# Layer 0's query, attention-value and HGRN-gate projections as three products of halves, row by row of the weights

## The reference

```
(na_q, na_k, na_v, hq, hf, hb, hi, hg, ga, gh) = split_columns(h @ w_in)
slab of 512 columns:  0     1     2     3   4   5   6   7   8,9  10,11
o_na = neighbourhood_attention(rope(na_q), rope(na_k), na_v, context k and v)
o_hg = hgrn2_bidirectional(silu(hq), hi, gates from hf and hb)
y    = sigmoid(ga) * (o_na @ w_na_o) + sigmoid(gh) * ((rms_norm(o_hg) * silu(hg)) @ w_hg_o)
x    = x + g1 * (y @ w_out)
```

## Time and profile before

| what | value |
|---|---|
| median of 3 runs | 1620.96 us (1620.72 to 1624.62) |
| profiled execution, its own time | 1620.81 us |
| its span, first to last instruction | 1618.9 us |
| mean granted TensorE clock | 0.96 |
| PE busy | 1470.9 us, 91% |
| DVE, ACT, POOL busy | 853.9, 649.3, 239.4 us |
| norm and slab 3 on PE | 41.69 to 71.31 us |
| slab 2, rotations, slab 7 on PE | 249.71 to 308.1 us |
| layer 0 attention on PE | 308.2 to 385.4 us |

### The profile page before, as it was taken

The page is one execution under the profiler, slowest core; times in us unless marked ns, Lnnn a source line. Parts: engine busy times, 40 slices in busy tenths (PEclk is TensorE's granted clock), DMA queues, the critical chain, the costliest instruction groups (busy, mean ns, idle before and its releaser), DMA issues.

```text
span 1618.9 us, 17176 instructions
## 1 busy us (share of the span) xinstructions
PE 1470.9 (91%) x6712; PEld 999.4 (62%) x6712; DVE 853.9 (53%) x1153; ACT 649.3 (40%) x880; POOL 239.4 (15%) x210
## 2 busy tenths in 40 slices
PE   3999999998999958999999789999889988998884
PEld 1586665456888836888888478765558864433332
DVE  3367971676744456888888356870871132111003
ACT  3554431257233255778877365430350121111112
POOL 0006951300000001111210210660500000000000
PEclk9999999999999967999999889999999998999997
DMA  9511106394121546999999861116342466999991
GB/s 354 208 52 52 53 15 183 144 387 156 52 104 56 205 156 223 391 400 400 399 400 403 296 257 52 53 53 156 135 178 101 145 222 226 392 395 393 395 394 65
DMA packets 167144, 352.12 MB, mean 218 GB/s; under 512 B 21776, under 2 KB 22928, under 8 KB 167056
## 3 DMA queue, kind: packets, MB, share of 16 engines
q1 hardware_dynamic: 145472, 331.52, 55.1%
q0 software_dynamic: 3456, 12.58, 2.1%
q10 hardware_dynamic: 18128, 6.82, 2.1%
HBM read 339.38 MB, written 11.53 MB: 217 GB/s over the span
## 4 chain that ended last, share of the span: by engine, by line
PE 79%; DVE 8%; DMA 4%; issue 3%; POOL 3%; ACT 2%; SPq 0%; DVEq 0%; ACTq 0%; POOLq 0%
PE bank L1237 7%; PE bank L579 6%; PE bank L669 4%; PE bank L1259 4%; PE bank L989 4%; PE bank L986 4%; PE bank L995 3%; PE bank L590 3%; PE bank L615 3%; DMA ring<-in_w_in 2%; PE bank L806 2%; PE bank L809 2%; PE bank L802 2%; PE bank L1014 2%; PE bank L1024 2%
## 5 line engine op out<-in xcount | busy, mean ns | idle before, releaser
L2754 DVE TENSOR_TENSOR slab_lo<-slab,high 128x4096 fp32r<-128x4096 f32 x48 | 212.0, 4419 | 8.2 <-ACT high L1898 7.5
L1898 ACT ACTIVATE high<-slab 128x4096 fp32r<-128x4096 f32 x48 | 174.1, 3632 | 22.5 <-PE bank L995 14.5
L1237 PE MATMUL bank<-narrow_slab,picked 128*64 128x512 f32 x256 | 116.0, 607 | 12.0 <-issue 11.7
L1238 PE MATMUL bank<-narrow_slab,picked 128*64 128x512 f32 x256 | 116.2, 608 | 0.0
L2184 POOL DMA_INDIRECT feed_rows<-token_table,slot_token x16 | 40.6, 2538 | 504.5 <-DVE slot_token L2694 305.9
L669 PE MATMUL bank<-hT,ring 128*128 128x512 f32 (+1 forms) x256 | 102.8, 539 | 0.0
L579 PE MATMUL bank<-hT,ring 128*128 128x256 f32 (+1 forms) x384 | 99.6, 415 | 0.0
L579 PEld LDWEIGHTS bank<-hT,ring 128*128 128x128 f32 x384 | 72.9, 190 | 23.4 <-issue 15.1
L1237 PEld LDWEIGHTS bank<-narrow_slab,picked 128*64 128x64 f32 x256 | 35.2, 140 | 83.4 <-issue 82.8
L2920 DVE TENSOR_TENSOR hidden<-bank,gated 64x512 f32<-64x512 f32 x16 | 11.1, 695 | 121.1 <-ACT gated L2056 121.1
L1739 ACT ACTIVATE gsig<-bank 128x512 f32<-128x512 f32 (+1 forms) x32 | 15.7, 491 | 139.8 <-PE bank L579 69.9
(11 more groups left out here) (330 smaller groups left out, 3012.4 us busy)
## 6 DMA issues: line engine op xcount, KB each, us to landing
ring<-in_w_ada SPq DMA_DIRECT2D x24, 2048.0 KB, 13.3
ring<-in_w_in SPq DMA_DIRECT2D x24, 2048.0 KB, 8.8
slab<-in_w_gate SPq DMA_DIRECT2D x16, 2048.0 KB, 15.3
slab<-in_w_up SPq DMA_DIRECT2D x16, 2048.0 KB, 14.5
slab<-in_w_down SPq DMA_DIRECT2D x16, 2048.0 KB, 14.2
narrow_slab<-in_w_gate SPq DMA_DIRECT2D x16, 2048.0 KB, 17.4
narrow_slab<-in_w_up SPq DMA_DIRECT2D x16, 2048.0 KB, 22.0
narrow_slab<-in_w_down SPq DMA_DIRECT2D x16, 2048.0 KB, 19.2
```

The costliest lines, as they stand in the source:

```text
L1237: T.matmul(bank[0][0:64, :], x, gate[:, k, :], start=(k == 0), stop=(k == KT - 1))
L1238: mm = T.matmul(bank[0][64:128, :], x, up[:, k, :], start=(k == 0), stop=(k == KT - 1))
L1898: S.activation(half_of(e, kind)[:], w[:], ACT.Copy)\
L2754: V.tensor_tensor(low[:], w[:], half_of(e, kind)[:].bitcast(f32), ALU.subtract)\
```

## The change

In layer 0 slabs 3, 2 and 7 are now done by halves and by rows of the weights, as slab 6 was. Two functions hold the PE side, `tokens_by_halves` (slabs 6 and 2) and `features_by_halves` (slabs 3 and 7). Both open their four banks before the first product. The high rows lie in small buffers: 4 for slab 3, 4 for slab 2, 7 for slab 7.

- For slab 3, ACT and DVE now make a tile of `hT`, its high half, its low half, and the high and low half of the weight row, before they go on to the next tile. `levmask` moves ahead of the norm.
- `hT_hi` is made by ACT right after HGRN's last unit, and `hT_lo` by DVE before the rotations (in place over `hT`). The copies inside attention and ahead of the wide gates are gone, and `wide_gates` takes the tiles in plain order.
- DVE makes the low rows of slab 2 and the first three of slab 7 before the rotations, and the other five of slab 7 one each ahead of the first five rotations. ACT makes the last five high rows of slab 7 behind the four copies of slab 2's results.
- The 32 bias DMAs go from ACT's queue to SP's, ahead of the fill for the seventh ada slab, in both layers.
- Some buffers move: `ona`, `merged`, `pt`, `probs` 4 and 5. ACT waits for all eight heads of `bias` before its first write of `pt`, where DVE waited before it wrote `probs` 4 and 5.

```diff
+    query_row = [fixed(f"query_row{i}", [P, TOK], f32r, offset=A0 + 2 * KB * i) for i in range(4)]
-    hT_hi = fixed("hT_hi", [P, KT, TOK], f32r, offset=B0)
+    hT_hi = fixed("hT_hi", [P, KT, TOK], f32r, offset=A0 + 24 * KB)
+    values_row = [... for i in range(4)]
+    hgate_row = [... for i in range(7)]
...
+            def features_by_halves(l, s, who, hi, lo, there=None):
+                outs = [open_bank(("in", l, s, c), who) for c in range(4)]
+                for k in range(KT):
+                    key, _, w_low, w_high = near_row(l, s, k)
+                    pe.wait_ge(sem["way_high"], way_no(l, s, k))
+                    for x, name in ((hi, "tile_high"), (lo, "tile_low")):
+                        if there is not None:
+                            pe.wait_ge(sem[name], there + k + 1)
+                        for c, o in enumerate(outs):
+                            mm = T.matmul(o[:, :], w_high[:, c * P:(c + 1) * P], x[:, k, :], start=(k == 0 and x is hi), stop=False)
+                    mm.then_inc(sem["row_over"], 1)
+                    pe.wait_ge(sem["way_low"], way_no(l, s, k))
+                    for c, o in enumerate(outs):
+                        mm = T.matmul(o[:, :], w_low[:, c * P:(c + 1) * P], hi[:, k, :], start=False, stop=(k == KT - 1))
...
+                if l == 0:
+                    tokens_by_halves(0, 2, "nav_ready", hT_hi, hT_lo, KT)
...
-                pe.wait_ge(*full(("in", l, 7)))
-                for c in range(4):
-                    project(l, 7, c, "hgate_ready", lo)
+                if l == 0:
+                    features_by_halves(0, 7, "hgate_ready", hT_hi, hT_lo)
...
+                    if loads[n] == ada_loads[(6, 22)[l]]:
+                        sp.wait_ge(*is_ready(("o", l, HG_HEADS - 1)))
+                        for r in range(4):
+                            ...
+                                sp.dma_start(bias_skew[...], skew).then_inc(sem["bias_loaded"], 16)
...
+                def row_high(s, k):
+                    key, w, _, high = near_row(l, s, k)
+                    if k == 0:
+                        act.wait_ge(*full(key))
+                    used = k - (5 if s == 6 else 7 if s == 7 else 4)
+                    if used >= 0:
+                        act.wait_ge(sem["row_over"], over_no(l, s, used))
+                        act.wait_ge(sem["way_low"], way_no(l, s, used))
...
+                    elif s == 7 and k >= 3:
+                        act.wait_ge(*is_ready(("in", l, 2, 3)))
...
-                norm(2 * l, 0)
+                norm(2 * l, 0, None if l else tile_low)
...
+                if l == 0:
+                    dve.wait_ge(*is_ready(("in", 0, 1, 3)))
+                    for k in range(KT):
+                        dve.wait_ge(sem["tile_high"], KT + k + 1)
+                        V.tensor_tensor(hT_lo[:, k, :], hT[:, k, :], hT_hi[:, k, :].bitcast(f32), ALU.subtract)\
+                         .then_inc(sem["tile_low"], 1)
+                    for s, ks in ((2, range(4)), (7, range(3)), (2, range(4, KT))):
+                        for k in ks:
+                            row_low(s, k)
                 for n in range(8):
+                    if l == 0 and n < 5:
+                        row_low(7, 3 + n)
                     dve.wait_ge(*is_ready(("rot", l, n)))
```

More of the change, by code:

```diff
@@ L488, in near_chunk, with row_home, near_row, rows_in_order @@
             return key, chunk_of(slot(key), KT, n % 4), chunk_of(slot_low(key), KT, n % 4), near_hi[n % 2]
[L490 to L492 removed]
+        def row_home(s, k):
+            return query_row[k % 4] if s == 3 else values_row[k % 4] if s == 2 else hgate_row[k % 7] if s == 7 else row_hi[(0, 1, 2, 3, 4, 0, 1, 2)[k]]
+        def near_row(l, s, k):
+            key = ("in", l, s)
             whole, low = [x.rearrange("p (k n) -> p k n", k=KT)[:, k, :] for x in (slot(key), slot_low(key))]
[L494 to L496 removed]
+            return key, whole, low, row_home(s, k)
+        def rows_in_order():
+            order = []
+            order += [(0, 3, k) for k in range(KT)]
+            order += [(0, 6, k) for k in range(KT)]
+            order += [(0, 2, k) for k in range(4)] + [(0, 7, k) for k in range(3)]
+            order += [(0, 2, k) for k in range(4, KT)] + [(0, 7, k) for k in range(3, KT)]
+            order += [("gates", n) for n in range(16)]
+            return order + [(1, 6, k) for k in range(KT)]
+        row_order = rows_in_order()
+        def way_no(*which):
+            return row_order.index(which) + 1
+        def over_no(l, s, k):
+            return [(0, 3), (0, 6), (0, 2), (0, 7), (1, 6)].index((l, s)) * KT + k + 1
+        chunks_before, tiles_before = (0, 8 + 24), (0, 3 * KT)
         def gate_chunk(n):
@@ L724, in _ @@
                     break
-                pe.wait_ge(*full(("in", l, 2)))
-                for t in range(4):
-                    project_rows(l, 2, t, "nav_ready")
+                if l == 0:
+                    tokens_by_halves(0, 2, "nav_ready", hT_hi, hT_lo, KT)
+                else:
+                    pe.wait_ge(*full(("in", l, 2)))
+                    for t in range(4):
+                        project_rows(l, 2, t, "nav_ready")
                 for n in range(8):
@@ L735, in _ @@
                         .then_inc(sem["psum_ready"], 1)
-                pe.wait_ge(*full(("in", l, 7)))
-                for c in range(4):
-                    project(l, 7, c, "hgate_ready", lo)
+                if l == 0:
+                    features_by_halves(0, 7, "hgate_ready", hT_hi, hT_lo)
+                else:
+                    pe.wait_ge(*full(("in", l, 7)))
+                    for c in range(4):
+                        project(l, 7, c, "hgate_ready", lo)
                 pe.wait_ge(sem["rope_done"], 8 * (l + 1))
@@ L798, in wide_gates @@
                         pe.wait_ge(sem["chunk_high"], 8 + n + 1)
-                        for i, k in enumerate(first):
-                            if n == 0 and k in (2, 0):
-                                pe.wait_ge(sem["tile_high"], KT + (8, 0, 6)[k])
-                            T.matmul(o[:, :], high[:, k, :], hT_hi[:, k, :], start=(i == 0), stop=False)
-                        for i, k in enumerate(first):
-                            if n == 0 and k in (2, 0):
-                                pe.wait_ge(sem["tile_low"], KT + (8, 0, 6)[k])
+                        for k in range(KT):
+                            T.matmul(o[:, :], high[:, k, :], hT_hi[:, k, :], start=(k == 0), stop=False)
+                        for k in range(KT):
                             T.matmul(o[:, :], high[:, k, :], hT_lo[:, k, :], start=False, stop=False)
@@ L1702, in _ @@
                             keep_beside()
+                if l == 0:
+                    for k in range(KT):
+                        S.activation(hT_hi[:, k, :], hT[:, k, :], ACT.Copy).then_inc(sem["tile_high"], 1)
                 while extra:
                     keep_beside()
+                if l == 0:
+                    for k in range(4):
+                        row_high(2, k)
                 for h in range(HG_HEADS):
@@ L1723, in _ @@
                     S.activation(navv[:, t, :], result(("in", l, 2, t))[:, :], ACT.Copy).then_inc(sem["nav_ready"], 1)
+                if l == 0:
+                    for k in range(3, KT):
+                        row_high(7, k)
                 for c in range(4):
```

179 lines of the change are left out of this document (90 added, 89 removed).

## The result

| | kernel before | changed kernel |
|---|---|---|
| median of 20 runs each | 1620.84 us (1616.33 to 1624.62) | 1623.69 us (1619.47 to 1627.96) |
| ratio, 95% interval | | 1.0020 (1.0012 to 1.0028) |
| span of the profiled execution | 1618.9 us | 1619.6 us |
| PE busy | 1470.9 us | 1453.8 us |

PE works 17.1 us less and the kernel is 3.2 us slower by the ratio (1.9 to 4.5), against a forecast of +6.1. That is clear of zero, but less than the 4.9 us that the prediction would call a change. The profiled execution of the changed kernel took 1621.42 us, 2.3 us less than the median of its runs, while that of the kernel before took its median. The two traces are therefore only 0.7 us apart, and what the other 2.5 us were in the untraced runs is not shown.

A forecast was written before the change was run, and what follows sets the result against it. PE, busy 91% of the span, was taken to bound the kernel. Terms +0.1 (slab 3), +6.2 (slabs 2 and 7), -0.2 (attention) and 0 (layer 1) gave +6.1 us, so 1627 us; range 1615 to 1631 us.

The forecast's parts named there:

- Slab 3: Layer 0's slab 3: a closed loop of ACT and DVE takes 3.73 us a tile, giving +0.1 us instead of -5.3.
- Slab 2: Layer 0's slab 2: PE sets the pace at 2.77 us a row, -5.3 us; rotation products over at 275.3 us.
- The wait before slab 7: Before layer 0's slab 7, PE stands still 14.2 us until DVE's fourth rotation, at 4.5 us a rotation beside POOL.
- The low clock: Behind the wait before slab 7, PE restarts at the low granted clock and loses 2.6 us.
- Attention: Layer 0's attention: ACT and DVE lose 8 copies and 8 subtractions, -0.2 us, bounds 0 and -1.
- Layer 1: Layer 1 costs 0 and keeps its gap of 5 us before the first attention product.
- Bias DMAs from SP: Bias DMAs on SP at ACT's 0.705 us each: POOL starts within a tenth of where it did, value 0.
- C: Bias comes later from SP, POOL starts about 9 us later, rotations 0 to 3 undisturbed; 1612 us, chance 0.08.
- D: Bias comes earlier from SP, POOL starts some 8 us earlier, layer 1 loses its gap; about 1622 us, chance 0.07.
- Rival A: Before slab 7: the wait for four banks is cheaper, a rotation costing 3.4 us; 1623.7 us, chance 0.15.
- Rival B: Slab 3: PE sets the pace after all, -4.4 us in place of +0.1; 1622.4 us, chance 0.12.
- Rival E: Slabs 3, 2 and 7: the change delivers its arithmetic, -4.4, -5.3 and -5.3 us; 1605.8 us, chance 0.03.

The follow-up runs named there:

- eight products more: Changed kernel with eight added, overwritten PE products ahead of layer 0's first gate chunk; ratio 1.0036 to the kernel before.
- the repeat: The changed kernel measured once more, unaltered, beside the other experiments; 1622.25 us, ratio 1.0021 to the kernel before.
- four products more: Changed kernel with four added, overwritten PE products ahead of layer 0's first gate chunk; ratio 1.0040 to the kernel before.
- DVE's order in slab 3: Changed kernel with DVE issuing the next normed tile ahead of the previous low tile and low row in layer 0's slab 3; 1617.08 us, ratio 0.9993.
- DVE's order after slab 2: Changed kernel with DVE doing rotations 0 to 3 before slab 7's low rows 3 to 6; 1613.36 us, ratio 0.9964 to the kernel before.
- only its layer 1 is edited: Kernel before with layer 1's rotation products 0 to 3 issued ahead of slab 2; 1611.13 us, ratio 0.9954.
- POOL kept out: Changed kernel with POOL starting layer 0's bias only after all eight rotations; 1616.74 us, ratio 0.9988 to the kernel before.
- the mends: Changed kernel, layer 0: next normed tile issued first in slab 3, rotation products 0 to 3 ahead of slab 2; 1603.26 us, ratio 0.9894.

## Why the prediction was right, and which terms were not

- **The likeliest case was the one that came.** Slab 7 waits for four rotations, the closed loop eats slab 3, slab 2 delivers. Measured was +3.2 us by the ratio (slower by 0.12 to 0.28%), forecast +6.1. The time, 1623.7 us, is 3.3 us under the 1627 and within the range of 1615 to 1631, but just under the 1624.5 to 1630 that the forecast gave itself, and within the 0.3% where it had set 0.44. That the total is no further off is in part luck. In the two traces the change costs +1.5 us up to attention and +1.5 in it, which the later stages nearly cancel.
- **Slab 3** (+0.1 us): the loop was forecast at 3.73 us and is 3.72, the end at 71.4 and is 71.31. What the step did not have is that the loop has no slack for a late start.
- **Slab 2** (-5.3 us): 2.72 us a row instead of 2.77, rotation products over at 274.8 instead of 275.3. Right, but most of this half microsecond came before it: slab 2 begins at 249.14 us, not at 249.71. The stretch from slab 4 to the first `o` product takes 167.6 to 167.7 us in all kernels with a split slab 3 and 168.0 to 168.1 with a plain one, which the forecast did not have.
- **The wait before slab 7** (14.2 us) is the mis-sized term; it is 11.29. The price of a row and rotation beside POOL was right, 4.49 us measured and 4.5 forecast. What was wrong is how many of them stand beside POOL. DVE began 0.85 us earlier than I had it (273.26, not 274.1) and POOL 0.75 later (276.61, not 275.86), so two pairs out of four went undisturbed instead of one. 4.49 - 1.74 = 2.75 us of the error is that one pair. How the two engines fall beside each other differs between executions: 12.39 us in the kernel with eight products more.
- **The low clock** (2.6 us): slab 7 takes 309.65 - 286.04 = 23.61 us where eight rows are 21.8, so 1.8 us. The clock was back some 3 us after the first product, sooner than in the two rows I took the earlier trace rows, and so it was in the repeat. With the same instructions up to here, the kernel with four products more lost 3.2 us (24.97), so the 2.6 is a fair middle. Together, +6.2 became 309.65 - 308.19 = +1.5 us.
- **Attention** (-0.2 us): it is +1.48, 78.67 instead of 77.19 us. Behind the 3.10 us gap, which is still 3.10, the granted clock is 0.72 from 382 to 387 us, where it was 1.00 before, and the products after the gap are slow:

```profile
380.82 1.68 PE L823 MATMUL bank<-const,probs 128*128 128x128 f32 x8 [3.10 <-DVE probs L2639]
382.43 1.98 PE L834 MATMUL bank<-pt,navv 128*64 128x256 f32 x8
```

  The first eight took 1.22 us before. In three of the experiments (DVE's order in slab 3, DVE's order after slab 2, four products more) they take 1.22 again and the stage 77.1 us. The last of them has the changed kernel's instructions up to here. In turn the kernel before takes 78.74 us for the stage when only its layer 1 is edited. So the +1.48 us is not shown to be the change's, and neither is any cost or gain of the missing copies.
- **Layer 1** (0): its gap is 5.05 us as forecast, against 4.96. The later stages were set at 0. In the two traces they moved by +0.27 us (layer 0's gates), -1.65 (from its second norm to layer 1's attention), +1.94 (layer 1's attention), 0 (its branches), -2.36 (from its second norm to its first expert) and -0.44 (the rest). That is -2.2 us in all, which with the +2.9 up to the end of layer 0's attention leaves the +0.7 of the spans. That they nearly cancel is luck.
- **Bias DMAs from SP** (0): 32 in 21.14 us, 0.66 us each against ACT's 0.705. They left the queue 1.8 us earlier (270.66 against 272.48 us), and yet POOL starts 0.75 us later; why is open. Rivals C and D fall. What C would have made of layer 0 can be seen with POOL kept out: the fourth rotation is done at 281.0 us, where C had 281.8.
- **Rival A** gave 1623.7 us, the measured time, from a price that isn't there: 3.4 us for each pair beside POOL, where 4.49 was measured. A total alone would have confirmed it. **Rival B** (PE sets slab 3's pace) is what the kernel with the exchanged order does, and there it gave 5.4 us in its stage and 4.4 in the whole. **Rival E** came true only with the mends.
- **The lock of the port.** The Trainium skill, page "SBUF — State Buffer", section "SBUF: two separate sides", has the loser of the shared port pair blocked for the other's whole instruction. The estimate by it was 5.1 us for a pair; the trace's 4.49 is below it here too. The full bill of POOL's company is 2.75 us a pair.

## What to carry to other kernels

Before splitting a product, write down for each engine the round from one tile to the next and look for an instruction that stands behind a wait and is itself waited for: here one line of DVE decided over 4.4 us. Work that needs all its banks at once waits for the slowest of their readers, so count whose banks they are, and move the readers ahead rather than making them faster. An effect of under 4 us in this kernel is judged by where its own stage ends, and in more than one trace, since untouched stages differ by as much from one execution to another.

## What the runs showed of the hardware that was not expected

- A stage with its instructions in the same order has other lengths in other executions. Layer 1's attention took 54.98 and 54.99 us in the two traces of the changed kernel, and 51.83 to 56.59 us in kernels edited elsewhere; layer 0's took 77.1 to 79.6, and the way from layer 1's second norm to its first expert 26.9 to 29.3. The granted clock fell in some and stayed in others, at equal idle times of PE (3.09 to 3.10 us in layer 0).
- The granted clock came back 3.1 us after PE's first product in two traces and 6.1 us after it in a third, behind the same wait of 11.29 us before slab 7.
- DVE's low row took 0.68 us alone and 1.74 to 1.76 us beside POOL, 1.06 us more; a rotation's multiply took 1.48 us behind such a row and 1.30 behind a rotation. DVE's reading of a bank beside POOL took 0.41 us, as when alone.
- The 32 small DMAs of layer 0 left SP's queue in 21.14 to 21.16 us in the kernels with a split slab 3 and in 22.00 and 22.33 in the two with a plain one, against 22.57 and 22.41 from ACT's. In layer 1 they took SP 22.5 to 24.1 us. The queue alone doesn't set their pace.
